# A second copy of x laid out by feature, unnormed first products, and each token's root applied where the sums are read

## What is computed

```
h    = x * rsqrt(mean(x*x, axis=-1) + EPS) * pre_mix_norm
proj = h @ w_in                        # att_q, att_k, att_v, gdn_qkv, gdn_z, gdn_a, gdn_b
gdn_qkv = silu(causal depthwise conv of width 4 over tokens)
o_att   = attention of 8 heads with a relative bias (one block of 256 keys)
o_gdn   = gated delta rule over chunks, q and k of it l2-normalized, gated by silu(z)
mix  = concat(o_att, o_gdn) @ w_out;  x = x + rms_norm(mix) ...
```

## Time and profile before

| | |
|---|---|
| median of 3 executions | 912.13 us (911.82 to 912.15) |
| the profiled execution: its own time | 912.35 us |
| its span in the trace | 910.5 us |
| PE busy | 898.0 us, 99% |
| DVE, ACT, POOL busy | 602.7, 461.4, 90.9 us |
| chain that ended last | PE 80%, DVE 12%, ACT 4% |
| mean rate of the DMA | 176 GB/s |

### The profile page before, as it was taken

The page is one execution under the profiler, slowest core; times in us unless marked ns, Lnnn a source line. Parts: engine busy times, 40 slices in busy tenths (PEclk is TensorE's granted clock), DMA queues, the critical chain, the costliest instruction groups (busy, mean ns, idle before and its releaser), DMA issues.

```text
span 910.5 us, 12778 instructions
## 1 busy us (share of the span) xinstructions
PE 898.0 (99%) x5466; PEld 765.9 (84%) x5466; DVE 602.7 (66%) x705; ACT 461.4 (51%) x558; POOL 90.9 (10%) x92
## 2 busy tenths in 40 slices
PE   9999999999999999999999999999999999999997
PEld 8989888888888887888888878778788888888886
DVE  6889985777666557687867565555656666564665
ACT  7765554555444446645444255453355555454443
POOL 2142100100000000000125310110100000000000
PEclk9999999999999999999999999999999999999999
DMA  8734523244555554544565534454454356445531
GB/s 325 281 108 177 174 67 117 93 162 185 188 193 198 200 199 179 220 164 161 185 231 185 185 123 188 152 185 166 163 202 163 139 177 236 175 183 223 185 139 47
DMA packets 24218, 159.81 MB, mean 176 GB/s; under 512 B 3241, under 2 KB 3769, under 8 KB 5857
## 3 DMA queue, kind: packets, MB, share of 16 engines
q1 hardware_dynamic: 21600, 152.58, 45.8%
q0 software_dynamic: 2272, 6.24, 2.0%
q10 hardware_dynamic: 288, 0.17, 0.1%
HBM read 157.91 MB, written 2.63 MB: 176 GB/s over the span
## 4 chain that ended last, share of the span: by engine, by line
PE 80%; DVE 12%; ACT 4%; issue 2%; DMA 0%; POOL 0%; POOLq 0%; DVEq 0%; ACTq 0%
PE banks L494 31%; PE banks L462 20%; PE banks L465 10%; DVE t_wl L1582 4%; PE banks L434 4%; PE banks L585 3%; PE banks L522 2%; PE banks L739 2%; PE banks L993 2%; PE banks L405 1%; ACT t_wh L1114 1%; DVE t_hold L1600 1%; DVE t_xt L1600 1%; PE banks L943 1%; PE banks L1075 1%
## 5 line engine op out<-in xcount | busy, mean ns | idle before, releaser
L1582 DVE TENSOR_TENSOR t_wl<-t_raw,t_wh 128x2048 fp32r<-128x2048 f32 x139 | 318.0, 2309 | 123.2 <-ACT t_wh L1114 121.9
L462 PE MATMUL banks<-t_hx,t_wh 128*128 128x512 f32 x992 | 312.0, 396 | 0.0
L1114 ACT CAST t_wh<-t_raw 128x2048 fp32r<-128x2048 f32 x139 | 261.5, 1906 | 12.8 <-DMA t_raw<-in_W 8.1
L465 PEld LDWEIGHTS banks<-t_hx,t_wl 128*128 128x128 f32 x992 | 186.3, 188 | 43.8
L465 PE MATMUL banks<-t_hx,t_wl 128*128 128x256 f32 x992 | 194.9, 278 | 0.0
L462 PEld LDWEIGHTS banks<-t_hx,t_wh 128*128 128x128 f32 x992 | 153.3, 189 | 2.4
L494 PE MATMUL banks<-t_wh,t_hx 128*128 128x512 f32 x320 | 102.3, 396 | 0.0
L494 PEld LDWEIGHTS banks<-t_wh,t_hx 128*128 128x128 f32 x320 | 59.5, 188 | 12.7 <-issue 0.6
L494 PE MATMUL banks<-t_wl,t_hx 128*128 128x512 f32 x160 | 61.1, 390 | 0.0
L434 PE MATMUL banks<-t_hx,t_wh 128*128 128x256 f32 x336 | 60.6, 285 | 0.4 <-ACT t_hx L1157 0.4
L2187 POOL TENSOR_TENSOR t_st<-t_st,t_half 128x1 f32<-128x1 f32 (+1 forms) x18 | 10.6, 589 | 432.5 <-DVE t_st L1608 430.7
(11 more groups left out here) (310 smaller groups left out, 1265.5 us busy)
## 6 DMA issues: line engine op xcount, KB each, us to landing
t_raw<-in_W SPq DMA_DIRECT2D x143, 1024.0 KB, 4.8
skew<-scr POOLq DMA_DIRECT2D x1, 1536.0 KB, 16.3
t_x<-in_x SPq DMA_DIRECT2D x2, 512.0 KB, 4.8
t_tab<-in_tab POOLq DMA_DIRECT2D x1, 640.0 KB, 7.1
out<-t_xt SPq DMA_DIRECT2D x2, 320.0 KB, 2.3
t_raw<-in_W SPq DMA_DIRECT2D x1, 512.0 KB, 6.9
t_T<-skew POOLq DMA_DIRECT2D x4, 128.0 KB, 2.5
t_xt<-skew POOLq DMA_DIRECT2D x4, 128.0 KB, 2.4
```

The source lines that it names most:

```text
L462: e.matmul(bank[b + c], M.wh[:, h, wk], M.hx[:, k, :, :].rearrange("p a s -> p (a s)"), start=k == 0, stop=False)
L465: m = e.matmul(bank[b + c][:, 0:S], M.wl[:, h, wk], M.hh[:, k, :], start=False, stop=k == 7)
L1114: e.copy(M.wh[:, h, 0:n], M.raw[:, r, 0:n]).then_inc(q.sem, q.tick(("hi", i)))
L1582: e.tensor_tensor(M.wl[:, h, 0:n], M.raw[:, r, 0:n], M.wh[:, h, 0:n].bitcast(F32), ALU.subtract).then_inc(q.sem, q.tick(("lo", i)))
```

## The change

- `t_xT`, a second copy of x, feature-major with pre_mix_norm in front, is prepared outside and loaded in two pieces, first of all, into the room of `t_cout`. The first four weight units are loaded and split in halves. SP's order is now: xT first piece, Z first half, xT second piece, Z second half, unit 1, ident, small, half of unit 2, x (two tiles), and on.
- `turn_x` with scaling and transposing is gone. ACT and DVE write the parts from xT with pre_mix_norm multiplied in (`leading_of_tokens`, `trailing_of_tokens`); 9 constant products stand ahead instead of 14 + 4 + 1. Z's 24 products are reordered.
- The squares of x are taken later, between the halves of units 2 and 3. `roots()` in the middle of conv 1 spreads the roots over the partitions by two products, ACT copies them to `t_rbc` (128 x 256).
- The root is multiplied in: for the gates by DVE (4 small operations for 2); for conv 0 and conv 5 by DVE straight from PSUM (`scaled`); for conv 1 to 4 ACT copies as before (now named "cq") and GpSimd multiplies `t_cin` by `t_rbc` in place ("cin"), upon which ACT's first tap waits; for z and the values through the scale of ACT's reading; for qk 0 to 3 ACT copies and GpSimd multiplies in place ("qs").
- The attention's bias product moves from before Z to the middle of conv 0. The cumulated gate sums move from behind conv 1 to behind conv 2; the SiLUs of conv 0 and 1 from u = 2 to u = 3.

The diff, cut to its core:

```diff
+SPLIT = 4
+BY_VECTOR = (0, 5)
...
+        M.rbc = sb(p1, "rbc", [128, S])[:]
...
+        M.xT = cout1[:, 0:8 + 8 * S]
...
-            constants(14)
-            turn_x("in")
-            b = take("bias", 0)
+            constants(9)
+            x_in = lambda k: q.wait_ge(DV, ("xl", "in", k))
+            b, i = take("ab", 1), next_unit()
             opened(b)
-            q.wait_dma(LD["onehot"])
-            q.wait_dma(LD["rbT"])
-            e.matmul(bank[b][0:8, 0:384], M.rb, M.oh, start=True, stop=True).then_inc(q.sem, q.tick("bias"))
-            drain(b, DV, "row")
-            constants(1)
-            x_in = lambda k: q.wait_ge(DV, ("xl", "in", k))
-            b_unit("ab", x_in, AC, "ab", "Z", to=1, halved=True)
+            steps = [(k, n) for n in range(3) for k in range(4)] + [(k, n) for n in (0, 2, 1) for k in range(4, 8)]
+            for k, n in steps:
+                q.wait_ge(*((DV, ("lo", i, k // 4)) if n == 2 else (AC, ("hi", i, k // 4))))
+                q.wait_ge(*((DV, ("xl", "in", k)) if n == 1 else (AC, ("xh", "in", k))))
+                w, a = ((0, 0), (0, 1), (1, 0))[n]
+                m = e.matmul(bank[b][:, 0:S], W[w][:, i % HR, k * 128:k * 128 + 128], H[a][:, k, :],
+                             start=(k, n) == steps[0], stop=(k, n) == steps[-1])
+            m.then_inc(q.sem, q.tick("ab", ("unit", i)))
+            drain(b, AC, "ab")
+
+            def bias_row():
+                b = take("bias", 0)
+                opened(b)
+                q.wait_dma(LD["onehot"])
+                q.wait_dma(LD["rbT"])
+                e.matmul(bank[b][0:8, 0:384], M.rb, M.oh, start=True, stop=True).then_inc(q.sem, q.tick("bias"))
+                drain(b, DV, "row")
+
+            def roots():
+
+                b = take("roots")
+                opened(b)
+                q.wait_dma(LD["ident"])
+                for t in range(2):
+                    q.wait_ge(PO, ("rstd", "in", t))
+                    m = e.matmul(bank[b][:, t * 128:t * 128 + 128], M.ms[:, t:t + 1].broadcast_to([128, 128]), ident[:],
+                                 start=True, stop=True)
+                m.then_inc(q.sem, q.tick("roots"))
+                drain(b, AC, "rbc")
...
+                bias_row()
...
-                b_unit(("conv", u), x_in, AC, ("cin", u), halved=u == 0,
-                       mid=gates if u == 0 else queries_and_keys if u == 5 else None)
-                if u == 1:
+                b_unit(("conv", u), x_in, *((DV, ("cin", u)) if u in BY_VECTOR else (AC, ("cq", u))), halved=u < 3,
+                       mid=gates if u == 0 else roots if u == 1 else queries_and_keys if u == 5 else None)
+                if u == 2:
...
-                q.wait_ge(AC, ("qk", 3))
+                q.wait_ge(PO, ("qs", 2 + p // 2))
...
-            e.dma_start(ident[:], A["ident"]).then_inc(LD["ident"], 16)
-            e.dma_start(M.small[:, 0:NSM], A["small"]).then_inc(LD["small"], 16)
+            def leading_of_tokens(*ks):
+                for k in ks:
+                    q.wait_dma(LD["xTa"])
+                    if k >= 4:
+                        q.wait_dma(LD["xTb"])
+                    e.activation(M.hh[:, k, :], M.xT[:, 8 + k * S:8 + k * S + S], ACT.Copy,
+                                 scale=M.xT[:, k:k + 1]).then_inc(q.sem, q.tick(("xh", "in", k)))
+
+            leading_of_tokens(0, 1)
+            hi_half(0, 1024)
+            leading_of_tokens(2, 3, 4, 5)
+            hi_half(1, 1024)
+            leading_of_tokens(6, 7)
+            hi_halves()
+            q.wait_ge(PE, "ab")
+            e.copy(M.ab, bank[at["ab"]][:, 0:S]).then_inc(q.sem, q.tick("ab"))
+            hi_half(0)
             for t in range(2):
                 q.wait_dma(LD[f"x{t}"])
                 square_of(M.x[:, t, cols(1)], M.xpart[:, 2 * t + 1:2 * t + 2], ("xsq", "in", t, 1))
-                scale_x("in", t)
-            hi_halves(1024)
-            turn_x("in", par("pre_mix"))
-            hi_halves()
-            next_unit()
-            q.wait_ge(PE, "ab")
-            e.copy(M.ab, bank[at["ab"]][:, 0:S]).then_inc(q.sem, q.tick("ab"))
+            hi_half(1)
+            hi_half(0)
+            q.wait_ge(PE, "roots")
+            e.copy(M.rbc, bank[at["roots"]][:, 0:S]).then_inc(q.sem, q.tick("rbc"))
+            hi_half(1)
+            unit[0] += 1
...
-                q.wait_ge(PE, ("conv", u))
-                e.copy(M.cin[:, 2 * u:2 * u + 2, 3:], halves(bank[at["conv", u]][:])).then_inc(
-                    q.sem, q.tick(("cin", u)))
-                q.wait_ge(q, ("cin", u))
+                if u in BY_VECTOR:
+                    by = DV
+                else:
+                    by = PO
+                    q.wait_ge(PE, ("conv", u))
+                    e.copy(M.cin[:, 2 * u:2 * u + 2, 3:], halves(bank[at["conv", u]][:])).then_inc(
+                        q.sem, q.tick(("cq", u)))
+                if u > 2:
+                    if u == 3:
+                        silu_of(0)
+                        silu_of(1)
+                    silu_of(u - 1)
+                q.wait_ge(by, ("cin", u))
                 q.wait_ge(PO, "pad")
                 for i in range(2):
                     a = 2 * u + i
                     e.activation(M.cout[:, a, :], M.cin[:, a, 0:S], ACT.Copy,
                                  scale=cw[:, a, 0:1]).then_inc(q.sem, q.tick(("tap", a, 0)))
-                if u == 1:
+                if u == 2:
                     q.wait_ge(DV, "gc")
                     e.activation(M.eg, M.gcum, ACT.Exp).then_inc(q.sem, q.tick("eg"))
                     q.wait_ge(DV, "kdx0")
                     e.activation(M.kdx, M.kdx, ACT.Exp).then_inc(q.sem, q.tick("kdx"))
-                elif u:
-                    if u == 2:
-                        silu_of(0)
-                    silu_of(u - 1)
-                    if u == 5:
-                        silu_of(5)
+                elif u == 5:
+                    silu_of(5)
...
+            trailing_of_tokens(0, 1)
             lo_half(0, 1024)
+            trailing_of_tokens(2, 3, 4, 5)
             lo_half(1, 1024)
-            turn_x("in", par("pre_mix"))
+            trailing_of_tokens(6, 7)
             lo_half(0)
             lo_half(1)
             q.wait_ge(PE, "bias")
             q.wait_dma(LD["neg"])
             tt(M.rrow, bank[at["bias"]][0:8, 0:384], M.ng, ALU.add, "row")
-            next_unit()
+            lo_half(0)
+            squares(0)
+            squares(1)
+            lo_half(1)
+            unit[0] += 1
...
+            def scaled(u):
+                q.wait_ge(PE, ("conv", u))
+                q.wait_ge(AC, "rbc")
+                tt(M.cin[:, 2 * u:2 * u + 2, 3:], halves(bank[at["conv", u]][:]), rep(M.rbc, 2), ALU.mult, ("cin", u))
+
+            scaled(0)
+            lo_half(1)
...
+            for u in range(6):
+                if u not in BY_VECTOR:
+                    o = M.cin[:, 2 * u:2 * u + 2, 3:]
+                    q.wait_ge(AC, ("cq", u))
+                    q.wait_ge(AC, "rbc")
+                    tt(o, o, rep(M.rbc, 2), ALU.mult, ("cin", u))
+
+            def scaled(u):
+
+                o = (M.qT, M.kTa)[u // 2][:, 2 * (u % 2):2 * (u % 2) + 2, :]
+                q.wait_ge(AC, ("qk", u))
+                tt(o, o, rep(M.rbc, 2), ALU.mult, ("qs", u))
...
             q.wait_ge(AC, ("kT", 1, 2))
             q.wait_ge(AC, "kdx")
             tt(heads(M.kd), heads(M.tm[:, 0, 512:1024]), bc(M.kdx[:, 0:8], 64), ALU.mult, "kd")
+            scaled(1)
+            scaled(2)
             q.wait_ge(DV, "ab_")
-            for h in range(2, 8):
+            load_T(2)
+            load_T(3)
+            scaled(3)
+            for h in range(4, 8):
...
+            a = 8 + 4 * S
+            e.dma_start(M.xT[:, 0:a], A["xT"][:, 0:a]).then_inc(LD["xTa"], 16)
+            half_of(0, 0)
+            e.dma_start(M.xT[:, a:a + 4 * S], A["xT"][:, a:a + 4 * S]).then_inc(LD["xTb"], 16)
+            half_of(0, 1)
+            half_of(1, 0)
+            half_of(1, 1)
+            e.dma_start(ident[:], A["ident"]).then_inc(LD["ident"], 16)
+            e.dma_start(M.small[:, 0:NSM], A["small"]).then_inc(LD["small"], 16)
+            half_of(2, 0)
             for t in range(2):
                 e.dma_start(M.x[:, t, :], A["x"][t * 128:t * 128 + 128, :]).then_inc(LD[f"x{t}"], 16)
-            weights(0)
-            for i in range(1, len(PLAN)):
+            half_of(2, 1)
+            half_of(3, 0)
+            half_of(3, 1)
+            for i in range(SPLIT, len(PLAN)):
```

99 lines of the change are left out of this document (51 added, 48 removed).

## The result

The changed kernel takes **933.51 us** (median of 4 runs, 932.61 to 935.03) beside 912.11 (911.82 to 912.15) on the same chip: a ratio of 1.0237 with a 95% interval of 1.0224 to 1.0250. It is slower by 21.4 us. The profiled execution took 933.19 us, with a span of 931.4. First the page: busy time by engine, and the chain that ended last by engine, the lines that answer to the earlier trace rows.

What follows compares the result with a forecast made beforehand. PE, busy 898.0 of 910.5 us, bounds the kernel. To 912.35 were added 17.3 up to the attention (3.8 gain already used up), 1.5 for q and k and 1.2 for clock: 932.3, median 932, range 922 to 938.

Steps and rivals of the forecast that it cites:

- the clock's 1.2: PE's clock falls in its waits before conv 4 (return hidden) and in z, where its return costs 1.2 us.
- First product at about 6.2: Start of PE: Z's first product at about 6.2 us, against 11.94 before.
- conv 0 at 10.4: Z's 24 products, paced by ACT, let conv 0 begin at 10.4 us against 15.29, a gain of 4.9.
- gain by then 3.8: After PE's added bias and root products, conv 4 could begin at 38.9 us for 42.70, 3.8 earlier.
- Skew is issued at 23.5: GpSimd, after roots, table and tiny copy, issues the copy to skew at 23.5 us, against 22.10 before.
- It took 16.3 us to land: 39.8: Skew's transfer takes 16.3 us as before, so its data land at 39.8 us.
- Done at 43.4: GpSimd's multiplication of conv 1, behind skew's landing and four loads, takes 1.1 us and ends at 43.4.
- steps 1 to 4: From conv 1's multiplication to conv 5's SiLU: conv 4 starts 5.8 us later, conv 5 8.9, its SiLU 17.3.
- steps 2 and 3: Conv 2, with GpSimd waiting for DVE's 2.3 us operation, and conv 3: conv 5 starts 8.9 later; DVE ends unit 8 at 72.5.
- What comes on top: Beyond the 17.3 us: GpSimd's multiplications of q and k holding DVE, 1.5 from 0 to 3.3, and 1.2 for PE's clock.
- The rule that was weighed: GpSimd and two-SBUF-input DVE operations exclude each other; taken for multiplications, not roots; held strictly, the sum would be 934 us.
- GpSimd is free in time: Rival: skew lands by 30.2 us, the early start's gain survives to conv 4's end, 910.3 us at best; chance 5%.

Runs made afterwards that it cites:

- run 5: Changed kernel with GpSimd's tiny copy of the bias row to DRAM issued before the two roots of x, loads still ahead of the multiplications: 932.08 us.
- run 8: Changed kernel with products of constants in PE's waits, 44 before conv 4 and 13 before the transposes of v: 933.03 us.
- Run 9: The kernel of run 7 with 20 products of constants ahead of the transposes of v: 917.74 us.
- runs 3 and 4: Changed kernel with GpSimd's multiplications of conv 1 to 4 left out: 918.61 us; with those of q and k left out too: 914.48 us.
- run 1: Changed kernel with GpSimd's loads from skew moved behind its four multiplications of conv 1 to 4: 919.39 us.
- run 10: The kernel of run 9 with DVE multiplying every conv block straight from PSUM, ahead of its trailing part: 915.19 us.
- run 7: The kernel of run 1 with ACT taking the cumulated sums' exponentials later, beside the decay's: 917.70 us.

## Why the prediction was right, point by point

932 us was predicted and 933.5 measured, within the range of 922 to 938, by the mechanism that was named: GpSimd's multiplication of conv 1 behind the loads from skew. That the number is so near is in part luck. Against the kernel before, in the spans: SiLU of conv 5 19.4 for 17.3, q and k 2.1 for 1.5, PE's products behind SiLU 0.7 for the clock's 1.2, and 1.3 given back at the end, for which nothing had been taken. Its steps:

- **"First product at about 6.2", "conv 0 at 10.4", "gain by then 3.8".** 6.59 and 11.36 measured. ACT waited for the second piece of xT until 7.71, which the forecast had taken as there in time; the gain at conv 0 is 3.9 instead of 4.9. PE was through with the decay's products at 40.0, for 42.70 before, so "gain by then 3.8 us" was 2.7. As forecast, it was lost in the next part.
- **"Skew is issued at 23.5".** Wrong by 4.7: 28.20. Two terms were mis-sized. The roots ended at 20.08 instead of 18.4: the squares were there at 18.5, 0.7 late, and the two roots took 0.94 and 1.35, where 0.55 each was taken; beside them lie DVE's second square and a trailing half. And the tiny copy took 7.28 with its issue, and 7.6 with the wait, where 4.5 was taken. The added megabyte and the weights in the queues may be why; it was not tried apart.
- **"It took 16.3 us to land: 39.8".** It took 13.57: 41.77. The two errors cancel in part, and run 5 shows that they belong together: issued at 22.31 it took 17.5. The transfer's time was no constant to be carried over; its landing moved by a third of its issue.
- **"Done at 43.4" and steps 1 to 4.** The loads of 0.57 to 0.53 were as forecast, the multiplication took 1.27 for 1.1: 45.53. From there the steps nearly kept their size: conv 4 8.1 later for the forecast's 5.8, with 2.1 of the difference there when the first multiplication ended (45.53 for 43.4); SiLU 19.4 later for 17.3, again 2.1. The waits of conv 2 and 3 for DVE's trailing part, 2.90 and 2.99 with the multiplication, stood in steps 2 and 3. PE's wait before the transposes of v was 3.2, not 6, since z began at 72.4 and not at 67.9: PE had waited 2.9 for the decay's rows before it.
- **"What comes on top": 1.5 for q and k.** Too small: 2.1. The three that meet DVE's SBUF work hold it for 3.2 in all, near the upper bound that was named (3.3), but the first is hidden behind PE's products, and the last two reach the triangle in full. The forecast had also said that nothing after 120 us gives time back, and 1.3 came back, 0.76 of it a wait of the kernel before that is absent now.
- **"The clock: 1.2".** From SiLU to DVE's reading of PSUM 0.7 are added, where PE works at 0.59 and then 0.98; with the constants of run 8 that reading comes at 104.04 for 104.29, 0.25 earlier, and between the medians 0.5 are won. Run 9 wins nothing. The clock did fall as forecast, but at conv 4 PE was not the bound, and behind SiLU DVE stood close behind it.
- **The rule that was weighed.** The Trainium skill (SBUF — State Buffer, on SBUF's two separate sides) has GpSimd and a DVE operation with two SBUF inputs exclude each other for a whole instruction. For multiplications the rows shown here agree: 1.27 alone, 2.52 to 3.0 beside a trailing part, and 1.0 to 1.1 taken from DVE's operation where GpSimd had the turn. For the root of 128x32 it does not: 5.46 us from 77.17, while DVE's six taps from 78.27 took 2.46 as always. That is how the forecast had taken it. Its question whether all three of q and k's that meet DVE's SBUF work are paid is answered by runs 3 and 4: DVE is held by all three, and two of them are paid.

What the forecast did not see is the size of what lies behind its main term. It put all of the 17.3 us down to the place of the multiplications behind skew. Of the 21.4 that place explains 14.1 (run 1). The other 7.3 are there without it, and only parts of them are known. GpSimd's multiplications behind the trailing parts are 2.5 (run 10 against 9). q and k's are 2.1 at the triangle. Moving the exponentials gave 1.7 (run 7), which the change needn't have caused. 2.9 stay in the best order tried, and q and k's multiplications are in them; what else is, and how much the early start takes off, was not run apart. The parts come from different bases and needn't add up.

The rival "GpSimd is free in time", at 910.3 with a loss of only 1.8 to 4.0 between conv 4 and conv 5's SiLU, would thus have been wrong even with its condition met: run 1 meets it and takes 919.4.
